# A decoder block's attention on one core: values, transposes and scores share points between half products, and gate loads and stores are queued ahead of HGRN2's last store

## What is computed

```
h = rmsnorm(x); proj = h @ w_in            # nine groups: sb q,k,v,z; hgrn q,f,i,z; gates (2 x 1024)
# stick-breaking attention, per head, tiles of 128 queries, strictly causal
z = q k^T / sqrt(128)
w = sigmoid(z) * product over later keys of sigmoid(-z)
sb_o = w @ v;         u_sb = (sb_o * silu(sb_z)) @ w_sb_proj
# HGRN2, chunkwise recurrence over 128-wide states, then RMS norm per head
f = lb + (1 - lb) * sigmoid(hg_f);  S = diag(f) S + (1 - f) i^T;  o = S^T silu(hg_q)
u_hg = (rmsnorm(o) * silu(hg_z)) @ w_hg_proj
y = sigmoid(gate_sb) * u_sb + sigmoid(gate_hg) * u_hg
out = rmsnorm(x + y @ w_out)
```

## Time and profile before

| | us |
|---|---|
| median of three runs | 1414.13 |
| profiled execution | 1411.06 |
| its span | 1409.3 |
| TensorE (PE) busy | 1343.4 (95%) |
| VectorE (DVE) busy | 935.4 (66%) |
| GpSimd (POOL) busy | 725.7 (51%) |
| ScalarE (ACT) busy | 584.6 (41%) |
| half products' share of the chain that ended last | 40% |

### The profile page before, as it was taken

One profiled execution on the slowest core, in us unless ns is written; L12 is line 12 of the kernel. 1 busy time (PEld: TensorE's weight loads), 2 busy tenths in 40 slices (PEclk: granted clock), 3 DMA queues, 4 the chain that ended last, 5 costly groups with the idle time before them and its releaser, 6 DMA issues.

```text
span 1409.3 us, 23093 instructions
## 1 busy us (share of the span) xinstructions
PE 1343.4 (95%) x8408; PEld 1117.7 (79%) x8408; DVE 935.4 (66%) x1066; ACT 584.6 (41%) x966; POOL 725.7 (51%) x488
## 2 busy tenths in 40 slices
PE   5689999999999999999999999998989899999998
PEld 4568888888878878888888887887878778788886
DVE  4827976976886886797696698687635345545323
ACT  8326346345435625635634543562444422101131
POOL 6655754565555564475466555555568713323210
PEclk8799999999999999999999999999999999999999
DMA  5121121111121131112111121113454456434502
GB/s 150 30 75 31 61 73 47 62 31 60 60 63 60 31 91 60 31 62 75 45 62 31 60 74 49 60 31 105 155 189 135 150 207 192 138 100 124 194 31 104
DMA packets 134349, 119.41 MB, mean 85 GB/s; under 512 B 10096, under 2 KB 116592, under 8 KB 134256
## 3 DMA queue, kind: packets, MB, share of 16 engines
q1 hardware_dynamic: 125040, 92.84, 20.9%
q10 hardware_dynamic: 9216, 25.17, 5.2%
HBM read 88.63 MB, written 29.36 MB: 84 GB/s over the span
## 4 chain that ended last, share of the span: by engine, by line
PE 75%; DVE 8%; POOL 6%; issue 4%; ACT 3%; DMA 2%; ACTq 0%; SPq 0%; DVEq 0%; POOLq 0%
PE banks L1544 40%; PE banks L1796 11%; PE banks L1818 6%; PE banks L1626 5%; PE banks L1602 3%; POOL b_lo L596 3%; DVE scT L1291 2%; PE banks L1616 2%; POOL b_sum L596 2%; ACT b_hi L686 1%; PE banks L1685 1%; DVE hk L1059 1%; DMA w_raw<-in_w_in 1%; PE banks L1660 1%; PE banks L1687 1%
## 5 line engine op out<-in xcount | busy, mean ns | idle before, releaser
L1544 PE MATMUL banks<-a_hi,b_hi 128*128 128x512 f32 x1120 | 464.6, 415 | 32.8 <-DVE a_lo L1059 11.3
L1544 PE MATMUL banks<-a_hi,b_lo 128*128 128x512 f32 x1120 | 443.2, 396 | 0.0
L1544 PE MATMUL banks<-a_lo,b_hi 128*128 128x512 f32 x1120 | 442.3, 395 | 0.0
L596 POOL TENSOR_TENSOR b_lo<-w_raw,b_hi 128x512 fp32r<-128x512 f32 x108 | 167.6, 1563 | 247.0 <-ACT b_hi L686 247.0
L1544 PEld LDWEIGHTS banks<-a_hi,b_hi 128*128 128x128 f32 x1120 | 213.7, 191 | 77.7 <-issue 28.0
L596 POOL TENSOR_TENSOR b_lo<-b_sum,b_hi 128x512 fp32r<-128x512 f32 x120 | 173.5, 1446 | 164.4 <-ACT b_hi L686 164.4
L1544 PEld LDWEIGHTS banks<-a_hi,b_lo 128*128 128x128 f32 x1120 | 213.1, 190 | 47.9
L1544 PEld LDWEIGHTS banks<-a_lo,b_hi 128*128 128x128 f32 x1120 | 214.5, 191 | 37.5
L1161 DVE TENSOR_TENSOR_SCAN kappa<-kappa 128x128 f32<-128x128 f32 (+3 forms) x64 | 95.0, 1484 | 100.7 <-ACT kappa L803 100.7
L686 ACT ACTIVATE b_hi<-b_sum 128x512 fp32r<-128x512 f32 x120 | 75.6, 632 | 161.1 <-POOL b_sum L596 160.9
L670 POOL TENSOR_TENSOR w_lo<-w_raw,w_hi 128x1024 fp32r<-128x1024 f32 x20 | 55.7, 2787 | 142.3 <-ACT w_hi L686 142.3
(11 more groups left out here) (194 smaller groups left out, 2507.5 us busy)
## 6 DMA issues: line engine op xcount, KB each, us to landing
w_raw<-in_w_in SPq DMA_DIRECT2D x72, 512.0 KB, 5.0
gate_d<-gate_out SPq DMA_DIRECT2D x16, 512.0 KB, 3.4
gate_in<-gate_d ACTq DMA_DIRECT2D x32, 256.0 KB, 2.7
x_tok<-in_x SPq DMA_DIRECT2D x8, 512.0 KB, 6.3
z_d<-z_out SPq DMA_DIRECT2D x8, 512.0 KB, 2.7
hz_d<-z_out SPq DMA_DIRECT2D x8, 512.0 KB, 2.7
osb_d<-o_sb SPq DMA_DIRECT2D x8, 512.0 KB, 6.0
ohg_d<-hq SPq DMA_DIRECT2D x8, 512.0 KB, 2.6
```

The costliest lines, as they stand in the source:

```text
L596: return nc.gpsimd.tensor_tensor(dst, a, b, op)
L1544: last = mm(bank, w[:, s, k, :], t[s][:, k, :], start=opens and k == 0 and z == 0, stop=k == QUAD - 1 and z == 2, skip_group_check=not opens)
```

## The change

Four tables move work between points: the transposes of tiles 0 to 3 go from points 3, 5, 7, 9 to 4, 6, 8, 10; the values of tiles 0 to 3 from 4, 6, 8, 10 to 6, 8, 10, 12; the copy of the first four output tiles from 10 to 13. At every point TensorE now does values, then transposes, then scores, where it did transposes, scores, values. Only the first parts of tiles 4 to 7 are still transposed ahead of a point's half product; ScalarE's copies follow the same rule. On SyncE's queue the fifth gate load (load_gate_pair(4)) and the store of gate pair 1's first half (store_gate(1, 0)) now stand ahead of the last HGRN2 store.

```diff
-TURN_AT = {3: (0, 0), 5: (1, 0), 7: (2, 0), 9: (3, 0), 12: (4, 0), 13: (4, 1), 15: (5, 0), 16: (5, 1),
+TURN_AT = {4: (0, 0), 6: (1, 0), 8: (2, 0), 10: (3, 0), 12: (4, 0), 13: (4, 1), 15: (5, 0), 16: (5, 1),
            18: (6, 0), 19: (6, 1), 21: (7, 0), 22: (7, 1)}
-PV_AT = {4: 0, 6: 1, 8: 2, 10: 3, 14: 4, 17: 5, 20: 6, 23: 7}
-FINISH_AT = {10: 0, 23: 1}
+PV_AT = {6: 0, 8: 1, 10: 2, 12: 3, 14: 4, 17: 5, 20: 6, 23: 7}
+FINISH_AT = {13: 0, 23: 1}
...
+def turned_first(j, part):
+
+    return j >= 4 and part == 0
...
             store_gate(0, 0)
             store_gate(1, 1)
+            load_gate_pair(4)
+            store_gate(1, 0)
             store_hg(HEADS - 1)
-            for g in range(2, N_GATE_PAIRS):
+            store_gate(2, 1)
+            for g in range(3, N_GATE_PAIRS):
...
-                    if u in TURN_AT and TURN_AT[u][1] == 0:
+                    if u in TURN_AT and turned_first(*TURN_AT[u]):
                         take_turned(h, *TURN_AT[u])
                     pair_point(pair, n, p)
...
-                    if u in TURN_AT and TURN_AT[u][1] == 1:
+                    if u in TURN_AT and not turned_first(*TURN_AT[u]):
                         take_turned(h, *TURN_AT[u])
...
-                    if u in TURN_AT and TURN_AT[u][1] == 0 and TURN_AT[u][0] >= 4:
+                    if u in TURN_AT and turned_first(*TURN_AT[u]):
                         turn(h, *TURN_AT[u])
                     project(pair, 4 * h + pair, u % PAIR_POINTS)
                     if u == V_AT:
                         turn_values(h)
-                    if u in TURN_AT and not (TURN_AT[u][1] == 0 and TURN_AT[u][0] >= 4):
+
+                    if u in PV_AT:
+                        attend_sb(h, PV_AT[u])
+                    if u in TURN_AT and not turned_first(*TURN_AT[u]):
                         turn(h, *TURN_AT[u])
                     if u in QK_AT:
                         scores(h, QK_AT[u])
-                    if u in PV_AT:
-                        attend_sb(h, PV_AT[u])
```

## The result

The changed kernel takes 1432.55 us (median of four runs, 1431.08 to 1434.74), the one before 1413.9 (median of four). The ratio is 1.0134, with a 95% interval of 1.0121 to 1.0147: slower by 18.7 us. The forecast was 1433 in a range of 1417 to 1442, slower with a chance of 0.88. The profiled execution took 1431.93 us with a span of 1430.2, and a mean granted clock of 0.978 (before: 0.986).

A forecast was written before the change was run, and what follows sets the result against it. TensorE, busy nearly all the time, was taken as the bound, so its idle time and work count. -12.2 + 25.3 + 10.5 - 4.3 = +19.3 on the profiled 1411.06 gives 1430.4, plus 3.07 to the median: 1433 us, range 1417 to 1442.

The forecast's parts named there:

- Sharing points: TensorE's points in the heads: merging groups of work saves nothing by itself, 0.5 us over the run at most.
- The first transpose: Point 3 to 4 in each head: half product covers the wait for VectorE's product, 1.53 us per head, -12.2 us.
- The stall: Point 14 in each head: TensorE waits 3.16 us for the output's first-half copy before tile 4's values, +25.3 us.
- The clock: TensorE behind those stalls: six in eight followed by the lower clock at 1.75 us each, +10.5 us.
- VectorE's later products: VectorE's products for tiles 4 and 7: still in time with 0.4 and 0.3 us spare, no cost taken.
- The gate stage: SyncE's queue: the earlier store removes ScalarE's 4.30 us gate sigmoid wait, handed on to the end, -4.3 us.
- Rival 1: Heads: the stall before tile 4's values comes but TensorE's clock doesn't fall, 1423 us; chance 0.20.
- Rival 2: Heads: the output's first-half copy is in time, so no stall, 1397.6 us; chance 0.08.
- Rival 3: Heads: VectorE's products for tile 4 or 7 become late too, 0.9 us per head, 1440 us; chance 0.10.
- rival 4: Heads: stall near 1.5 us cancels the gain, no slow clock, 1410 to 1415 us; chance 0.04.
- The sum: Whole run: terms total +19.3 us on the profiled 1411.06, plus 3.07 from profiled execution to median, 1433 us.

The follow-up runs named there:

- Experiment 4: Kernel before with only tile 0 moved (transpose to point 4, values to point 5, ahead of tile 1's transposes): 1401.44 us, ratio 0.9916.
- experiment 1: Changed kernel with the copy of the output's first half at point 12 instead of 13, ahead of the forget gate's activations: 1396.95 us, ratio 0.9887.
- experiment 2: Kernel before with only SyncE's queue changed (fifth gate load and gate pair 1's first-half store ahead of the last HGRN2 store): 1408.77 us, ratio 0.9970.
- experiment 6: Changed kernel with one more, unused activation of 1024 columns on ScalarE ahead of the copy of the output's first half: 1449.98 us, ratio 1.0255.
- experiment 5: Changed kernel with the scores of tile 6 ahead of the values of tile 4 at point 14: 1409.76 us, ratio 0.9976.
- experiment 7: Changed kernel with twelve needless matmuls of 512 columns ahead of TensorE's wait for the copy of the output's first half: 1421.74 us, ratio 1.0055.
- experiment 3: Changed kernel with SyncE's queue as before, so only the tables changed: 1438.38 us, ratio 1.0171.

## Why the prediction was right

- **Sharing points gives nothing by itself.** Right within the noise: the heads' gain is that of the first transpose alone. Experiment 4, which shares no points but one, takes 11.5 us off; experiment 1, with all the sharing and the queue's part, takes 16.0 off, of which the queue's part is 4.2 by experiment 2. 11.8 are left for the tables. Each of these has an interval of about 2 us either way, so a saving by sharing of that size isn't ruled out.
- **The first transpose, -12.2.** Right: 11.5 by experiment 4, and heads of 112.50 instead of 114.1 (1.6 each, 12.8 over eight) in experiment 1. In the first head the wait fell from 5.17 to 3.84, so the half product covered it there too.
- **The stall, +25.3.** Right in place, order and size. The forecast put it at 3.16 us per head. The transpose that starts at 590.02 and the half product behind it are over after 1.49, at 591.51, and the values start at 594.56, 3.05 later. The profile calls 2.88 of this idle, because it models the last matmul's end later. The forecast wait was 0.11 too long, mostly because the signal from the copy's end to TensorE was taken as 0.14 and is 0.05 here (594.51 to 594.56). A head that stalls is 3.17 longer than one of experiment 1 all the same, since the matmuls behind the stall start about 0.1 more slowly (scores 1.14 behind the values' start, against 1.04). That these two cancel is luck. Experiments 1 and 6 move the stall by the copy's place (0 and 3.82 as the profile counts) and experiment 5 by work put into it (1.55), and the time follows.
- **The clock, +10.5.** Right in kind; that the count came out as forecast is luck. Six of eight was a choice between none and all, not worked out; six of eight stalls were followed, at 2.0 us each and not 1.75, 12.3 together. That this is a cost of its own is shown by experiment 7 (10.8 less with the stall kept) and by 5, where the clock never fell. The Trainium skill's statement in TensorE: Matmul & The Clock Gate, section What's actually happening, that the point of change isn't tied to the kernel, agrees with this trace: of eight equal stalls of 2.88 us six were followed, and in experiment 3 another six.
- **VectorE's later products at nothing.** Right: there is no wait for them behind the first head, with the stall or without it.
- **The gate stage, -4.3.** 4.0 in the trace, 4.15 by experiment 2, 5.8 by experiment 3 against the changed kernel, where 1.4 us of the heads and another slow stretch are in the difference. As forecast, the wait was handed on to the next gate (1.81, where 3.57 stood) and the one near the end stayed (5.42 for 5.02). The moved store was in time: it went at 1038.61, and the sigmoid that needs it ran at 1049.38 without a wait.
- **The rivals.** Rival 1 (no slow clock) falls by the changed kernel's own windows; what it describes is experiment 7's time, 1421.74 for its 1423. Rival 2 (1397.6) is experiment 1: the time that the same tables give when the copy is in time, 1396.95. It decided at the point named. Rival 3 falls with the waits; rival 4 with the ratio.
- **The sum.** From one profiled execution to the other the change is +20.9 (12.6 + 12.3 - 4.0), from median to median +18.7; the forecast's +19.3 lies between. The profiled execution before was 3.07 below its median, the one after 0.6 below. So the closeness of 1433 to 1432.55 is partly luck: the clock's term was 1.8 too small, and the difference between a profiled execution and a median took that up.

## What to carry to other kernels

When work is moved on one engine, follow every instruction on the other engines that waits for it, and look at what stands ahead of that instruction in its own queue: here ScalarE, which works in order, had three activations, 3.4 us, between the copy of a transpose that had moved back and the copy for which TensorE waits. A change that removes a wait of 1.2 us can add one of 3.05 in the same head; one number in a table made the difference between 1.3% slower and 1.1% faster. Price a stall of the matrix engine with the clock that it may cost, which here was half as much again.

## What the runs showed of the hardware

- A stall of one length can be followed by the lower clock or not: 0 of 8 stalls of 1.55 us (experiment 5), 6 of 8 of 2.88 us (and 6 of 8 again in experiment 3), 8 of 8 of 3.82 us (experiment 6). The length alone doesn't decide it: in the first wait behind the gate stage, where TensorE had stood for about 5 us some 20 us earlier, waits of 1.84 us (experiment 4) and 1.97 us (experiment 3) were followed by the lower level (0.72 granted over the next 6 us), those of 1.57 to 1.78 us (experiments 5 and 2, changed kernel, kernel before) were not.
- Its price differs too. In the changed kernel heads were 117.3 to 117.5 us apart with a short stretch at the lower level and 118.4 to 118.5 with a long one, against 115.67 with none: 1.6 to 1.9, or 2.8 us.
- Matmuls whose results nobody needs, run in a wait that can't be avoided, kept the clock up and made the kernel 10.8 us faster (experiment 7). Taking the wait away made it 35.6 us faster (experiment 1).
